# The last expert's rows put back by TensorE, and five units of the second expert loaded early

## What is computed

```
scores = sigmoid(t @ router_w)                 # 384 x 16
# two experts per token, both of the best of 4 groups; weights sum to 1
top_w  = top_w / sum(top_w)
g = t @ w_gate[e];  u = t @ w_up[e]            # 16 experts, each 1024 x 1024
y = (silu(g) * u * combine[:, e]) @ w_down[e], summed over e
x = x + g2 * y
out = rms_norm(x, norm_final)
```

## Time and profile before

| | |
|---|---|
| median of 3 runs | 852.38 us |
| profiled execution | 851.2 us |
| its span, first to last instruction | 849.5 us |
| TensorE busy | 748.5 us (88%) |
| VectorE busy | 305.1 us (36%) |
| ScalarE busy | 185.2 us (22%) |
| GpSimd busy | 66.7 us (8%) |
| DMA, mean over the span | 305 GB/s, 259.15 MB |
| mean granted TensorE clock | 0.928 of full speed |

### The profile page before, as it was taken

One profiled execution on the slowest core, in us unless ns is written; L12 is line 12 of the kernel. 1 busy time (PEld: TensorE's weight loads), 2 busy tenths in 40 slices (PEclk: granted clock), 3 DMA queues, 4 the chain that ended last, 5 costly groups with the idle time before them and its releaser, 6 DMA issues.

```text
span 849.5 us, 22752 instructions
## 1 busy us (share of the span) xinstructions
PE 748.5 (88%) x9657; PEld 413.9 (49%) x9658; DVE 305.1 (36%) x884; ACT 185.2 (22%) x390; POOL 66.7 (8%) x98
## 2 busy tenths in 40 slices
PE   5699787878999979999998999999999999999830
PEld 5355463574644455554551654454553555445410
DVE  3889769998012263111120211111211211112017
ACT  3554242100022130112220112202201211221113
POOL 1000001920010002000000000000000000000000
PEclk9989898766999977999998999999999999999975
DMA  8900449940146762999999999999999999999933
GB/s 342 414 24 2 185 177 385 323 178 3 52 136 220 251 244 69 407 410 410 410 410 410 361 412 410 410 410 411 410 410 379 411 411 410 410 410 410 410 104 152
DMA packets 70011, 259.15 MB, mean 305 GB/s; under 512 B 10728, under 2 KB 10776, under 8 KB 65864
## 3 DMA queue, kind: packets, MB, share of 16 engines
q1 hardware_dynamic: 67352, 254.55, 76.4%
q0 software_dynamic: 1632, 3.20, 1.0%
q10 hardware_dynamic: 976, 0.67, 0.4%
HBM read 252.49 MB, written 6.29 MB: 305 GB/s over the span
## 4 chain that ended last, share of the span: by engine, by line
issue 54%; PE 13%; DVE 11%; POOL 3%; DMA 2%; POOLq 2%; ACT 1%; SPq 0%; DVEq 0%; ACTq 0%
PE ps L1044 5%; DVE sreg L1480 3%; PE ps L1104 3%; PE ps L996 3%; DVE scan_t L1472 2%; DVE scan_t L1473 2%; POOL y_scratch L511 1%; POOLq L529 1%; PE ps L1004 1%; DMA a4r<-slot_list 1%; POOL slot_list L485 1%; DMA ring<-y_scratch 1%; DMA sreg<-in_x_prompt 0%; DVE ring L1685 0%; DVE sreg L1674 0%
## 5 line engine op out<-in xcount | busy, mean ns | idle before, releaser
L1138 PE MATMUL ps<-ring,vreg 128*32 128x512 f32 x2240 | 250.3, 602 | 13.7 <-DMA ring<-in_moe_w_up 8.9
L1138 PEld LDWEIGHTS ps<-ring,vreg 128*32 128x32 f32 x2240 | 72.6, 111 | 184.2 <-issue 163.3
L1145 PE MATMUL ps<-ring,vreg 128*32 128x256 f32 x2240 | 124.2, 380 | 0.0
L1635 DVE TENSOR_TENSOR vreg<-vreg,ps 128x256 f32<-128x256 f32 x48 | 17.3, 416 | 227.5 <-ACT vreg L755 227.5
L1130 PEld LDWEIGHTS ps<-vreg,sreg 128*128 128x128 f32 x768 | 88.2, 192 | 13.4 <-issue 13.4
L1145 PEld LDWEIGHTS ps<-ring,vreg 128*32 128x32 f32 x2240 | 71.2, 110 | 46.8
L1130 PE MATMUL ps<-vreg,sreg 128*128 128x96 f32 x768 | 91.8, 276 | 0.0
L1646 DVE COPY vreg<-ps 32x256 f32<-32x256 f32 x96 | 40.7, 424 | 105.8 <-PE ps L1145 103.3
L767 ACT ACTIVATE vreg<-ps 32x256 f32<-32x256 f32 x96 | 35.8, 373 | 148.0 <-PE ps L1145 146.1
L755 ACT ACTIVATE vreg<-ps 128x256 f32<-128x256 f32 x48 | 15.0, 385 | 210.9 <-PE ps L1138 210.9
L1044 PE MATMUL ps<-ring 128*128 128x512 f32 x128 | 59.0, 620 | 1.4 <-issue 0.7
(11 more groups left out here) (271 smaller groups left out, 618.8 us busy)
## 6 DMA issues: line engine op xcount, KB each, us to landing
ring<-in_moe_w_gate SPq DMA_DIRECT2D x128, 512.0 KB, 12.8
ring<-in_moe_w_up SPq DMA_DIRECT2D x128, 512.0 KB, 14.2
ring<-in_moe_w_down SPq DMA_DIRECT2D x128, 512.0 KB, 12.3
ring<-in_w_ada SPq DMA_DIRECT2D x24, 1024.0 KB, 11.6
ring<-in_ssm_w_glu SPq DMA_DIRECT2D x8, 1024.0 KB, 15.5
ring<-in_ssm_w_in SPq DMA_DIRECT2D x8, 512.0 KB, 22.0
ring<-y_scratch SPq DMA_DIRECT2D x6, 512.0 KB, 6.3
tmat<-ada_rows SPq DMA_DIRECT2D x4, 512.0 KB, 5.6
```

Source lines behind the costliest of these rows:

```text
L1138: last = pe.matmul(ps[t][32 * j:32 * j + 32, :], xgT[:, k, 32 * t:32 * t + 32], w[:, :, 256 * j:256 * j + 256], start=(k == 0), stop=(k == ...
L1145: last = pe.matmul(ps[3 + t // 2][32 * dj:32 * dj + 32, 256 * (t % 2):256 * (t % 2) + 256], aT[:, t, c2, 32 * j:32 * j + 32], ring[:, KT + ...
```

## The change

Early units. The first five units of the second expert are loaded into five other places of on-chip memory as soon as these are free, in the order 4, 3, 0, 1, 2. VectorE copies each into its slot of the ring when TensorE has read the first expert's unit there. SyncE loads only units 5 to 11 of that expert itself. The gate rows g2 are now loaded behind the last weight.

Last expert. Its rows aren't scattered. After the last evictions TensorE multiplies `yrow` by `ohT_last`, the transposed one-hot matrix of the last expert with each token's weight in place of the one, so that each of the three token tiles gets its weighted rows in PSUM (six products of 96 x 128 by 96 x 512). VectorE multiplies them by the gate row and adds the sum of all else. That sum (`other_choice`) is made from the rows of the other 15 experts, which SyncE loads once 15 scatters have landed. `y2_d` is filled with zeros first, in six stores, so that rows never scattered add nothing. The one-hot matrix is made before the loop: `last_expert_rows` on VectorE, three transposes on TensorE, one copy on ScalarE. The slot numbers are computed later, behind the first evictions. On TensorE the gathers stand in conditionals, so that the last expert makes none.

```diff
+        early_unit = [mod2[:, 0, ...], mod2[:, 1, ...], h2T[...][:, 0:UNIT], tmat[...], front[:, :]]
+        y2c = [mod2 ..., h2T ...]          # both were in ring slots 4 to 6
+        zeros = route_flat[:, 0:D]
# SyncE
+            sp.wait_ge(pool_zeros, 1)
+            for t in range(2 * NT):
+                sp.dma_start(y2_d[t * P:(t + 1) * P, :], zeros).then_inc(st_zero, 16)
...
+            def load_early(u):
+                for h, w in enumerate((w_gate, w_up)):
+                    sp.dma_start(early_unit[u][:, h * D:(h + 1) * D], w[0, 1, u * P:(u + 1) * P, :]
+                                 ).then_inc(ld_early[u], 16)
+            load_early(4)
             sp.wait_ge(dve_x1, 6)
-            for cond in range(2):
-                load_rows(gate_rows[:, cond, :], cond, 2, 2, ld_g2)
-            with sp.Fori(1, NE) as e:
+            load_early(3)
+            sp.wait_ge(dve_h2, 6)
+            load_early(0)
+            load_early(1)
+            sp.wait_ge(pe_logit, NT)
+            load_early(2)
+            for u in range(len(early_unit), NU):
+                sp.wait_ge(unit_free, u + 1)
+                load_unit(u, 1)
+            with sp.Fori(2, NE) as e:
                 for u in range(NU):
                     sp.wait_ge(unit_free, e * NU + (u + 1 - NU))
                     load_unit(u, e)
-            sp.wait_ge(y_sent, 16 * NE)
+            for cond in range(2):
+                load_rows(gate_rows[:, cond, :], cond, 2, 2, ld_g2)
+            sp.wait_ge(y_sent, 16 * (NE - 1))
+            load_y2()                      # both choices of tiles 0, 1, 2
# POOL
+            pool.wait_ge(st_zero, 16 * 2 * NT)
-            with pool.Fori(0, NE) as e:
+            with pool.Fori(0, NE - 1) as e:
# ScalarE
+            act.wait_ge(st_zero, 16 * 2 * NT)      # ahead of scores(0, 2)
+            def first_choice(t, loads):
+                act.wait_ge(ld_y2[t], 32 * loads)
+                act.activation(y2c[0][:, t, :], y2c[0][:, t, :], ACT.Copy, scale=cmb[:, 0, t:t + 1]).then_inc(act_mo, 1)
             def expert(it, last=False):
...
+                if last:
+                    first_choice(0, 1)
+                    first_choice(1, 1)
                 act.wait_ge(unit_free, it * NU + NU)   # then the evictions of yrow
...
+            act.wait_ge(pe_oh_last, 1)
+            act.activation(ohT_last, ps[3][0:CAP, 0:NT * P]..., ACT.Copy).then_inc(act_oh_last, 1)
+            expert(NE - 1, True)
+            first_choice(2, 1)
# TensorE
-                gather_x(nth + 1, 0, 5)
+                with pe.If(e < NE - 1):
+                    gather_x(it + 1, 0, 5)
...
-                gather_x(nth + 1, 5, KT)
+                with pe.If(e < NE - 1):
+                    gather_x(it + 1, 5, KT)
...
+            pe.wait_ge(dve_oh_last, 1)
+            for t in range(NT):
+                last = pe.transpose(ps[3][0:CAP, t * P:(t + 1) * P], oh_last[:, t, :], ident[:])
+            last.then_inc(pe_oh_last, 1)
+            pe.wait_ge(act_oh_last, 1)
...
+            pe.wait_ge(y_ev, 12 * NE + 12)
+            for t in range(NT):
+                for half in range(2):
+                    last = pe.matmul(ps[2 * t + half][:, :], ohT_last[:, t, :], yrow[0:CAP, 512 * half:512 * half + 512],
+                                     start=True, stop=True)
+                last.then_inc(pe_back, 1)
# VectorE
             weights_of_choice()
+            last_expert_rows()             # 3 operations on 128x3, 2 on 128x288
...
+            slot_numbers()                 # was ahead of weights_of_choice
+            for u in range(len(early_unit)):
+                dve.wait_ge(ld_early[u], 32)
+                dve.wait_ge(unit_free, u + 1)
+                cp(ring[:, u, :], early_unit[u]).then_inc(ld_unit[u], 32)
...
+            def other_choice(t, loads):
+                dve.wait_ge(act_mo, NT * (loads - 1) + t + 1)
+                m = y2c[0][:, t, :]
+                stt(m, y2c[1][:, t, :], cmb[:, 1, t:t + 1], m, ALU.mult, ALU.add).then_inc(dve_mix, 1)
+                dve.wait_ge(dve_mix, 2 * (NT * (loads - 1) + t) + 1)
+                tt(m, m, gate_rows[:, 1 if t else 0, :], ALU.mult).then_inc(dve_mix, 1)
+                dve.wait_ge(dve_mix, 2 * (NT * (loads - 1) + t) + 2)
+                tt(m, m, x1[:, t, :], ALU.add).then_inc(dve_pre, 1)
# in the last expert, ahead of its evictions; other_choice(2, 1) stands behind them
+                if last:
+                    dve.wait_ge(ld_g2, 32)
+                    other_choice(0, 1)
+                    other_choice(1, 1)
...
             def combine(t):
-                dve.wait_ge(act_mo, t + 1)
-                step(stt(m_out[:, t, :], y2c[:, 1, t, :], cmb[:, 1, t:t + 1], m_out[:, t, :], ALU.mult, ALU.add))
-                step(tt(m_out[:, t, :], m_out[:, t, :], gate_rows[:, 1 if t else 0, :], ALU.mult))
-                tt(x1[:, t, :], x1[:, t, :], m_out[:, t, :], ALU.add).then_inc(dve_x2, 1)
+                dve.wait_ge(pe_back, t + 1)
+                for half in range(2):
+                    c2 = slice(512 * half, 512 * half + 512)
+                    step(tt(x1[:, t, c2], ps[2 * t + half][:, :], gate_rows[:, 1 if t else 0, c2], ALU.mult), half == 1)
+                tt(x1[:, t, :], x1[:, t, :], y2c[0][:, t, :], ALU.add).then_inc(dve_x2, 1)
+            dve.wait_ge(dve_pre, NT)       # ahead of combine(0)
```

More of the change, by code:

```diff
@@ L102, in build @@
         tmat = sb("tmat", [P, GP, L * GS])
-        ada = sb("ada", [P, 3, 512])
-        gains = sb("gains", [P, 512])
+        front = sb("front", [P, UNIT])
+        ada = front[:, 0:3 * 512].rearrange("p (b n) -> p b n", b=3)
+        gains = front[:, 3 * 512:UNIT]
         ident = sb("ident", [P, P])
@@ L225, in build @@
         ld_c = sem("ld_c")
-        ld_ada = [sem(f"ld_ada{i}") for i in range(len(ADA_SLOTS))]
-        ld_late = [sem(f"ld_late{i}") for i in range(NU)]
+        ld_piece = [sem(f"ld_piece{i}") for i in range(NU)]
         ld_win = [sem(f"ld_win{k}") for k in range(KT)]
@@ L256, in build @@
         st_list, st_out, st_scatter = (sem(n) for n in ("st_list", "st_out", "st_scatter"))
+        pool_zeros, st_zero, dve_oh_last, pe_oh_last, act_oh_last, dve_pre, pe_back, dve_oh_none, dve_mix = (sem(n) for n in (
+            "pool_zeros", "st_zero", "dve_oh_last", "pe_oh_last", "act_oh_last", "dve_pre", "pe_back", "dve_oh_none", "dve_mix"))
+        ld_early = [sem(f"ld_early{u}") for u in range(len(early_unit))]
         unit_free, ld_idx, oh_ready, xt_ps, xt_ev, silu_done, prod_done, at_ps, at_ev, y_ev, y_sent = (
@@ L410, in _, with load_y2 @@
                     load_unit(u, e)
-            sp.wait_ge(y_sent, 16 * NE)
+            for cond in range(2):
+                load_rows(gate_rows[:, cond, :], cond, 2, 2, ld_g2)
+            sp.wait_ge(y_sent, 16 * (NE - 1))
+            def load_y2():
+                for t in range(NT):
+                    for k in range(2):
+                        sp.dma_start(y2c[k][:, t, :], y2_d[k * T + t * P:k * T + (t + 1) * P, :]).then_inc(ld_y2[t], 16)
+            load_y2()
             v = sp.value_load(cmaxi[0:1, 0:1], min_val=0, max_val=T)
@@ L419, in _ @@
                 sp.wait_ge(y_sent, 16 * NE * ROUNDS)
+                sp.wait_ge(dve_pre, NT)
+                load_y2()
             sp.nop()
-            for t in range(NT):
-                for k in range(2):
-                    sp.dma_start(y2c[:, k, t, :], y2_d[k * T + t * P:k * T + (t + 1) * P, :]).then_inc(ld_y2[t], 16)
             for t in range(NT):
@@ L531, in _ @@
             with pool.If(v > CAP):
+                send(NE - 1, 0, NE - 1)
                 with pool.Fori(1, ROUNDS) as r:
@@ L750, in _, with expert @@
             scores(2, NT)
-            def expert(it):
+            def first_choice(t, loads):
+                act.wait_ge(ld_y2[t], 32 * loads)
+                act.activation(y2c[0][:, t, :], y2c[0][:, t, :], ACT.Copy, scale=cmb[:, 0, t:t + 1]).then_inc(act_mo, 1)
+            def expert(it, last=False):
                 for t in range(TT):
@@ L795, in ada_piece @@
                 b, k = divmod(n, KT)
-                if b == 0:
-                    pe.wait_ge(ld_ada[n], 16)
-                else:
-                    pe.wait_ge(ld_late[LATE_SLOTS[n - KT]], 16 * LATE_SLOTS[0:n - KT + 1].count(LATE_SLOTS[n - KT]))
+                slot = (ADA_SLOTS + LATE_SLOTS)[n]
+                pe.wait_ge(ld_piece[slot], 16 * (ADA_SLOTS + LATE_SLOTS)[0:n + 1].count(slot))
                 src = ring[:, ADA_SLOTS[n] if b == 0 else LATE_SLOTS[n - KT], :]
@@ L1160, in third_down, with expert @@
                     down(kk, 2)
-            def expert(it, nth, count=None):
-                pe.wait_ge(xt_ev, nth * 2 + 2)
+            def expert(it, e, count=None):
+                pe.wait_ge(xt_ev, it * 2 + 2)
                 pe.wait_ge(prod_done, it * TT + TT)
@@ L1226, in _ @@
                 with pe.Fori(1, ROUNDS) as r:
-                    pe.wait_ge(xt_ev, r * (2 * NE + 2))
```

(13 more changed lines are left out.)

92 lines of the change are left out of this document (54 added, 38 removed).

## The result

The changed kernel took 849.73 us (median of 9 runs, 845.29 to 851.44), the kernel before 853.97 us in the 9 runs beside it (850.85 to 856.68). The ratio is 0.9948, 95% interval 0.9926 to 0.9970: 4.4 us less, between 2.6 and 6.3. Forecast were 7.8 us. The direction was right, the size too large; the difference lies at the edge of the 0.5% which the forecast took as the least that can be told from none.

The account below looks back on a forecast made before the run. The DMA stream at about 410 GB/s was taken to bound the expert loop. Loop -4.8 and tail -3.0 sum to -7.8 us, taking the median from 852.38 to 844.6; range 839.5 to 848, with the other cases 836 to 852.

Parts of the forecast that it names:

- the one of the stream: Expert loop: five units (13.0 us) moved forward less 8.6 us late start; 5.1 us ahead from the fifth expert on.
- late start: Second expert's stream: DMA stands 8.6 us until the sixth unit's slot is freed, instead of starting at the first.
- The fifth expert's wait: Fifth expert's gate/up: TensorE waits only 0.9 us for its last unit, and gate/up ends 5.4 us earlier.
- The low clock: Fifth expert: the stretch at granted clock 0.50 (1.2 GHz) that followed the gaps goes.
- The DMA's dip at the full ring: Loop at 481 to 487 us: 1.5 us of idle DMA time is no longer idle.
- The start: Start of the loop: three more transposes and a ScalarE copy cost +0.8 us, bounds 0 and +2.
- The copies: First expert: VectorE's five copies into the ring take 2.4 us each and cost nothing.
- The conditionals: Around TensorE's gathers in each expert: 0 to 0.27 us each, up to 3.2 us in all, taken as +0.3.
- The third rival: TensorE's conditionals eat the 8.1 us gain from 0.68 us each; at 1.1 us the time is 857.5; chance 0.10.
- The tail: From the last weight to the last sum: last sum at 839.1 against 842.1, -3.0 us, bounds -1 and -6.
- One of the forecast's signs of being wrong: Last expert's down part: a dip of the clock there would show the forecast wrong; no size given.
- The first rival: Loop and tail: one part alone works, such as loop gaining 0.7 us and only the tail left; about 848.7; chance 0.20.

Follow-up runs that it names:

- early down units: The changed kernel with the second expert's down units 8 to 11 loaded early in place of units 0 to 4: 846.13 us, ratio to before 0.9918.
- the second pair of profiles: Kernel before and changed kernel each profiled once more, unchanged: first gather to last sum 522.2 us before, 517.1 us after.
- the two parts alone: Changed kernel without the early units: 849.45 us, 0.9958; kernel before with the five early units and gate rows behind the last weight: 852.21 us, 0.9993.
- the kernel with the evictions first: The changed kernel with the last expert's evictions ahead of the sums over the others, on ScalarE and VectorE: 846.11 us, ratio to before 0.9937.
- The last kernel: Changed kernel with down units 8 to 11 early, evictions first, and the one-hot transposes and copy moved into the last expert: 842.24 us, 0.9858 of before.

## Why the prediction was too large

**The step that failed** is the one of the stream: "Net -4.4, and with the later start -3.6 us", and 5.1 from the fifth expert on. Measured were 2.2 us at the fifth expert's eighth unit in one pair of profiles and nothing in the other, and 1.5 in the whole loop. I counted how long the DMA stands until the sixth slot is free, and took it as full from there. But its next three units are loaded faster than TensorE frees the fourth: between the end of gate/up and the first down slot lie 6 us of gathers and transposes and the first down products. In the kernel before the eight gate/up units, 21 us of transfers, bridged that time. Three don't. So: 13.0 us of units moved forward, less 7.7 of late start (23.1 - 15.4), less 2.3 of the second hole: 3.0. The eighth unit of the fifth expert landed 131.86 us behind the first gather (457.23 - 325.37) against 134.03: 2.2 us. The early down units, which have neither of these holes, gave 3.8 us in the loop.

The late start itself isn't fixed. It hangs on when TensorE has read six units of the first expert, and so on the clock there. In the second pair of profiles it is 9.6 us (24.9 - 15.3), close to the 9.4 of the forecast, and the second hole is 2.4 us: 1.0 is left, and the eighth unit lands at 133.7 in both kernels. The clock fell in the first expert's gate/up in both profiles of the kernel before, in the two other kernels without the early transposes, and in four of the eight profiles with them. Whether the transposes change its chance can't be said from so few.

**What hung on it.** The fifth expert's wait was to shrink to 0.9 us and the low clock to vanish. The wait stayed, since TensorE was still ahead of its units: 1.79 and 1.77 us stand before the eighth. The low clock stayed in the first profile (the row that begins with the eighth unit is even longer, 17.74 us against 16.72 in the earlier trace rows) and not in the second (14.80). The end of the fifth expert's gate/up was to come 5.4 us sooner behind the first gather; it came 1.1 sooner in the first pair and 2.0 in the second. The DMA's dip at the full ring was to be used up (1.5 us); in the first profile 0.34 x 2 + 0.10 x 2 = 0.9 us of it are left, in the second nothing. By these pieces the loop should have gained 2.8 us in the first pair; it gained 1.9, and the other 0.9 isn't assigned. In the second pair only the dip was gone, and it gained 1.1. That the two loops of the changed kernel agree (480.3 and 480.4) looks like luck: the second started 1.8 us later and had no fall of the clock in the fifth expert, the first had.

**The start.** Forecast +0.8 us, measured +1.2 (12.5 and 12.9 against 11.5 and 11.6), the transposes and the wait behind them: shown by the two parts alone and by the one-hot matrix turned later. The copies cost nothing, as forecast: with the early units alone the start is 11.6. Nor did the zero rows and the late slot numbers, which that kernel lacks: with the one-hot matrix turned later they are there, and the start is 11.7.

**The conditionals** cost nothing measurable: from the second expert's gate/up to the third's it is 27.38 us after and 27.42 before. The third rival is out.

**The tail** was right in each of its steps. Counted from the end of the last gate/up: first sum of VectorE forecast 15.0 (816.2 - 801.2), measured 14.7; end of the evictions 25.3, measured 24.9; last of the sums over the others 29.1, measured 28.8; last sum 37.9, measured 36.7. Of the 1.2 us at the end 0.3 were there before, and two terms make the rest. I took 0.7 us for products at the low clock. The first two ran low and the clock was up from the middle of the six, but VectorE hardly waited for them: its pause there is 0.36 us, and the same 0.36 stands in the kernel with the evictions first, where the products had ended 1.8 us before. And the three last sums took 7.5 us instead of 8.1, since two operations of 512 took 1.29 together and not 1.38. The tail gained 4.1 instead of 3.0. One of the forecast's signs of being wrong came all the same: the clock fell in the last expert's down part, in the second profile.

**The first rival**, one part alone works, comes nearest: I gave it 0.20 and a loop gain of 0.7. It named the right weakness (a gain that is a difference of larger numbers), with the wrong cause (rate, start, conditionals).

The last kernel holds what was left: 2.3 us by the other units, 2.9 by the order in the tail, 0.7 to 1.7 by the place of the transposes. Each is a difference of stretches of single profiles; the runs show the sum, 0.9858 against 0.9948.

## What to carry to other kernels

When part of a ring's load is moved ahead of a loop, follow the freed slots one by one to the end of the ring: move the units whose slots come free last, not first, so that the transfer can start at the first slot and doesn't run dry where the consumer does other work. What is queued ahead of an eviction in program order delays the engine that waits for it, however idle that engine is. Where the stages ahead of the change scatter by more than the gain, cut the profiles at a fixed event and compare the stretches, and look for a fall of the clock in each before the difference is put down to the edit.

## What the hardware showed

- A VectorE copy of 128x2048 f32 within on-chip memory took 1.23 us, about what its two-operand operations take for 1024 elements (1.22). The forecast had bounded it at 1.2 and 2.8 and taken 2.4. The Trainium skill, "VectorE: DVE Perf Modes" ("Mode 2×_2P — use both read ports for one tensor"), has two elements per cycle for a float32 copy whose source and destination are both in on-chip memory; the trace agrees.
- While these copies ran, POOL's indirect DMAs took up to 2.30 us each, against 0.97 to 1.07 before. By source line in the changed kernel:

```profile
L520 POOL DMA_INDIRECT slot_list<-sreg,h x6: 971/1410/2302, 340.1 to 349.8; - x6
```

The Trainium skill, "GPSIMD Engine Reference" ("8. Key points"), says that GpSimd shares its interfaces to on-chip memory with VectorE and contends with VectorE instructions in a 2-port perf mode. The runs agree: in the kernel with the tail only, which lacks the copies and has the same six indirect DMAs, each took 0.97 to 1.07 us, and so they did with the early down units, whose copies come 15 us later. It was hidden: behind its list POOL still waited 5.8 us for the first expert's rows.
- TensorE's granted clock fell to 0.50 (1.2 GHz) behind pauses of 0.8 to 2.3 us, in some executions and not in others of the same kernel: for the changed one in the first expert (15.39 us against 13.94), in the fifth (17.74 against 14.80) and in the last down part (8.80 against 7.31). It costs what TensorE's end is worth at that place: nothing in one order of the tail, 0.8 us in the other.
